# A two-block transformer on one NeuronCore: pool projections first on the unshifted input, the output projection in two halves, routing on the way

## The reference, cut to what matters

```python
ada = jax.nn.silu(c) @ w_ada[l] + b_ada[l]                    # 2048 x 12288 weights, one vector
sh1, sc1, gt1, sh2, sc2, gt2 = jnp.split(ada, 6, axis=-1)
h = modulate(rmsnorm(x, norm1_g[l]), sh1, sc1)                # xn * (1 + sc1) + sh1
proj = h @ w_in[l]
q, k, v, qi, ki, wi, p = jnp.split(proj, offsets, axis=-1)
q = rope_partial(rmsnorm(q, q_norm_g[l]), pos)                # 8 heads of 128; k has 2 heads
...
attn_out = dsa_attention(q, k, v, qi, ki, wi)                 # top-k of index scores masks the softmax
pool_out = multiscale_pool(p, w_pool[l], pool_scale[l])       # trailing mean minus identity, then a matmul
mix = jnp.concatenate([attn_out, pool_out], axis=-1) @ w_out[l]
x = x + gt1[:, None, :] * mix
h2 = modulate(rmsnorm(x, norm2_g[l]), sh2, sc2)
x = x + gt2[:, None, :] * hier_moe(h2, w_grp[l], w_exp[l], w1[l], w3[l], w2[l])
```

## Time and profile before

| | |
|---|---|
| median of three runs | 2413.72 us (2411.43 to 2416.28) |
| the profiled execution | 2411.38 us, its span 2409.1 us |
| TensorE busy | 2096.6 us (87%), mean granted clock 0.972 |
| VectorE, ScalarE busy | 1220.2 us (51%), 872.2 us (36%) |
| HBM read | 691.66 MB, 288 GB/s over the span |

### The profile page before, as it was taken

How to read it: one execution, slowest core, us unless ns; L and a number is a source line. 1 busy time by engine, 2 the same in 40 slices (tenths; PEclk the granted TensorE clock), 3 DMA queues, 4 the chain that set the end, 5 groups by cost and what they waited for, 6 DMA issues and landing times.

```text
span 2409.1 us, 38203 instructions
## 1 busy us (share of the span) xinstructions
PE 2096.6 (87%) x14478; PEld 1356.6 (56%) x14478; DVE 1220.2 (51%) x2209; ACT 872.2 (36%) x1339; POOL 32.8 (1%) x32
## 2 busy tenths in 40 slices
PE   5699998987988888888888888899989899997997
PEld 1377776872222222222222222798888899997887
DVE  1544786455443333333333333648865554477655
ACT  1333434442221111111111112547854444466543
POOL 0000000000000000000000000101100000000000
PEclk9899999998999999999999999999999999999998
DMA  9988785967999999999999999464345355543432
GB/s 383 403 313 295 256 291 201 320 233 287 422 422 422 422 422 422 422 422 422 422 422 422 422 422 420 148 232 140 123 149 183 123 175 184 176 147 101 139 127 93
DMA packets 135046, 695.44 MB, mean 289 GB/s; under 512 B 14992, under 2 KB 15120, under 8 KB 85264
## 3 DMA queue, kind: packets, MB, share of 16 engines
q1 hardware_dynamic: 134928, 693.81, 75.4%
HBM read 691.66 MB, written 2.10 MB: 288 GB/s over the span
## 4 chain that ended last, share of the span: by engine, by line
PE 50%; DMA 36%; DVE 6%; ACT 3%; issue 2%; SPq 2%; DVEq 0%; ACTq 0%
PE acc L1088 35%; DMA ring<-in_w 31%; DMA land<-in_stream_a 4%; PE acc L1085 3%; PE psS L1345 3%; PE psO L1139 2%; DVE WL L1793 1%; ACT WH L1499 1%; SPq L956 1%; DMA land<-in_stream_bc 1%; PE psM L1333 1%; PE acc L1333 1%; PE psT L1029 1%; ACT SB L1580 0%; PE psO L1369 0%
## 5 line engine op out<-in xcount | busy, mean ns | idle before, releaser
L1088 PE MATMUL acc<-HH,WH 128*128 128x256 f32 x2552 | 747.2, 293 | 32.9 <-DVE HL L1815 15.7
L1088 PE MATMUL acc<-HH,WL 128*128 128x256 f32 x2552 | 728.4, 285 | 0.0
L1088 PE MATMUL acc<-HL,WH 128*128 128x256 f32 x2552 | 727.8, 285 | 0.0
L1793 DVE TENSOR_TENSOR WL<-land,WH 128x1024 fp32r<-128x1024 f32 (+2 forms) x346 | 418.6, 1211 | 409.6 <-ACT WH L1499 405.3
L1088 PEld LDWEIGHTS acc<-HH,WH 128*128 128x128 f32 x2552 | 496.0, 194 | 75.2 <-issue 14.9
L1088 PEld LDWEIGHTS acc<-HH,WL 128*128 128x128 f32 x2552 | 496.4, 195 | 1.9 <-issue 1.0
L1088 PEld LDWEIGHTS acc<-HL,WH 128*128 128x128 f32 x2552 | 495.8, 194 | 0.0
L1499 ACT ACTIVATE WH<-land 128x1024 fp32r<-128x1024 f32 (+2 forms) x350 | 364.3, 1042 | 238.3 <-PE acc L1088 192.1
L1345 PE MATMUL psS<-ring,low 128*32 128x512 f32 x2048 | 276.6, 612 | 106.4 <-DMA ring<-in_w 105.4
L1345 PEld LDWEIGHTS psS<-ring,low 128*32 128x32 f32 x2048 | 40.8, 108 | 319.8 <-DMA ring<-in_w 289.7
L2172 DVE TENSOR_TENSOR X<-psM,X 128x512 f32<-128x512 f32 x128 | 88.5, 691 | 230.0 <-PE psM L1333 230.0
(11 more groups left out here) (343 smaller groups left out, 1899.0 us busy)
## 6 DMA issues: line engine op xcount, KB each, us to landing
ring<-in_w SPq DMA_DIRECT2D x384, 1024.0 KB, 26.5
land<-in_stream_a SPq DMA_DIRECT2D x284, 512.0 KB, 7.3
land<-in_stream_bc SPq DMA_DIRECT2D x246, 512.0 KB, 4.0
land<-in_stream_bc SPq DMA_DIRECT2D x12, 384.0 KB, 3.4
X<-in_xT SPq DMA_DIRECT2D x1, 2048.0 KB, 16.1
out<-low SPq DMA_DIRECT2D x4, 512.0 KB, 2.6
cst<-in_const SPq DMA_DIRECT2D x1, 1538.0 KB, 11.9
low<-in_w_pool SPq DMA_DIRECT2D x1, 1024.0 KB, 4.7
```

Of the source, the lines that this page charges most:

```text
L1088: mm = pe.matmul(bank[:, 0:S], w[:, kk, :], h[:, rows[kk], :], start=(z == 0 and i == 0), stop=stop)
L1793: ins = dve.tensor_tensor(wl, src, wh, ALU.subtract)
```

## The change

1. **ada order** is 4, 5, 6, 7, 0, 1, 2, 3, 8, ... (`ADA_FIRST`). After the four scale blocks and the sum of squares the eight pool projections run, on `HH0`/`HL0`: x times (1 + sc1) times gain, without the shift and without the token's norm. VectorE multiplies the token's norm into each result (`evac` of p); the shift adds the same to every position of a feature, which the pool maps to zero. Blocks 0 to 3 are spread among them, and `HH`/`HL` for the others are made meanwhile.
2. ki and wi share one projection (`kw`). The pool sums and `pmm` move among the qi projections.
3. The queries' norm is no longer multiplied into q: `qss` sums its squares into one column for each head, `qrms`/`qsqrt`/`qrec` are done once, and `soft` takes the result as a scale for each head (four instructions for each job in place of one).
4. `idx` uses two 64-row matmuls on one copy of the keys, into `psS`; one `idx` runs after the first half of a q projection, one after the second. Each `topk` is four steps of two rounds.
5. The output projection runs twice over all 16 outputs: first the pool half (`wp`), with the attention jobs among them, each result added to X, then the attention half (`wo`).
6. The router's weights are multiplied by the modulation (`cols`), and the logits are taken from the unnormed X after each `wo` (`logit`, 128x36), the norm and the shift's part (`shiftW`) being applied at the end. h2 is no longer made: `h2t` turns X, `pick` writes the token's norm into the choice matrix, and scale and shift are applied on the gathered tile by VectorE (`inputs`, two instructions of 512 elements in place of ScalarE's copy), in the loop too.
7. `place` ends before the list of tiles, which follows the first `pick`; `gt2rows` moves ahead of the last two `wo`. The first four `ring` slots are loaded as soon as the landing slots under them are free.

```diff
-    for b in range(8):
+    o.will_split([("p", n) for n in range(8)])
+    for g in range(4):
+        b = ADA_FIRST[g]
         for q in range(4):
...
+            if (g, q) == (3, 1):
+                first = o.halves_of["p", 0][0]
+                o.add("pe", "part", ("p", 0), 0)
...
+    for n in range(8):
+        o.proj(("p", n), between=shifts, first=int(n == 0))
...
+    for n in range(KD):
+        o.proj(("wp", n), halves=[o.halves_of["wo", n][0]], post="res", between=after if 0 < n < 14 else None)
+        if n == 0:
+            o.add("dve", "qrms")
+            o.add("act", "qsqrt")
+            o.add("dve", "qrec")
+        if n < 4:
+            topk(1, n)
+        if n in (2, 4, 6, 8):
+            o.job(n // 2 - 1)
+        if n == 13:
+            o.split_mix("wo", 0)
...
     for n in range(KD):
-        o.proj(("wo", n), post="res", between=after, first=int(n < 2))
+        o.proj(("wo", n), halves=[o.halves_of["wo", n][1]], post="res", between=last)
...
-    o.add("dve", "rstd", "wo")
-    o.acc.append(("router",))
-    for c in range(KD):
-        o.add("dve", "h2", c)
-        o.add("act", "h2", c)
-    o.add("dve", "gt2rows")
-    o.add("pe", "router")
-    o.add("act", "evac", ("router",))
-    o.add("pe", "routeT")
-    o.misc.append(("routeT",))
+    o.add("dve", "logits")
...
     o.add("dve", "place")
+    o.add("dve", "pick")
+    o.add("dve", "list")
+    o.add("dve", "weights")
...
+                        if name == "p":
+                            ins = dve.tensor_tensor(pooled(n // 2)[:, n % 2, :], bank[:, 0:S], RT, ALU.mult)
...
+            def inputs(i):
+
+                dve.wait_ge(moe["gt_full"], i + 1)
+                dve.tensor_tensor(XG, acc[1][:, :].rearrange("p (c n m) -> p c n m", c=4, m=CAP),
+                                  g2.rearrange("p (n c) -> p c n", c=4)[:, :, :, None].to_broadcast([P, 4, 4, CAP]),
+                                  ALU.mult).then_inc(moe["xg_half"], 1)
...
+                dve.tensor_tensor(XG, XG, sh2.rearrange("p (n c) -> p c n", c=4)[:, :, :, None].to_broadcast([P, 4, 4, CAP]),
+                                  ALU.add).then_inc(moe["xg_ready"], 1)
```

More of the change, by code:

```diff
@@ L413, in order_a @@
-    ada_t(7)
-    rest = [(("k", 0), "nr"), (("k", 1), "nr"), (("v", 0), None), (("ki", 0), "r"), (("wi", 0), None)]
-    rest += [(("qi", n), "r") for n in range(8)] + [(("q", n), "nr") for n in range(8)]
+            if g and q == 1:
+                scale_first(g - 1)
+            if g in (1, 2):
+                o.add("pe", "ssx", 4 * (g - 1) + q)
+            if (g, q) == (2, 3):
+                o.misc.append(("ssx", 7))
+                o.add("dve", "ssx", 7)
+                o.add("act", "sqrtx")
+                o.add("dve", "xr")
@@ new lines, in order_a, with topk, index, halfway @@
+    pool_at = {("kw", 0): 0, ("qi", 0): 1, ("qi", 2): 2, ("qi", 4): 3}
+    pmm_at = {("qi", 2): 0, ("qi", 4): 1, ("qi", 6): 2, ("qi", 7): 3}
+    def topk(qt, part):
+        o.add("dve", "topk", qt, part)
+    def index():
+        i = idx.pop(0)
+        o.add("pe", "idx", i)
+        o.add("act", "evac", ("idx", i))
+        o.add("dve", "idx", i)
+    def halfway(x):
+        calls = [0]
+        def step():
+            calls[0] += 1
+            if x != ("q", 7):
+                between()
+            if calls[0] == 1 and x[1]:
+                index()
+        return step if x[0] == "q" else between
@@ new lines, in order_a @@
+    for x, post in rest:
+        if x == ("q", 7):
+            while len(left) % 4:
+                ada(*left.pop(0))
+        o.proj(x, post=post, between=halfway(x))
+        if x in pool_at:
+            o.add("dve", "pool", pool_at[x])
+        if x in pmm_at:
+            for dc in range(2):
+                item = ("pmm", (pmm_at[x], dc))
+                o.add("pe", *item)
+                o.acc.append(item)
+                o.add("act", "evac", item)
+        if x[0] == "q":
+            index()
+            if x[1] >= 4:
+                topk(0, x[1] - 4)
@@ new lines, in order_a, with last @@
+    o.drain()
+    shared[0], owed[0] = False, 0.0
+    o.misc.append(("ssum", "wo"))
+    o.add("pe", "shiftW")
+    o.add("dve", "shiftW")
+    def last():
+        between(ADA_RATE[3])
+    for n in range(KD):
+        o.proj(("wo", n), halves=[o.halves_of["wo", n][1]], post="res", between=last)
+        if not left and ("adaT", 23) not in o.at["pe"]:
+            ada_t(23)
+            o.add("dve", "gt2rows")
+            o.add("pe", "gt2rows")
+            o.add("act", "gt2rows")
+    assert not left
@@ L737, in program @@
         X = sb("X", [P, KD, S])
+        low_at = (nc.sbuf_base + 31) // 32 * 32
         low = sb("low", [P, 48, S])
@@ L1702, in softmax_head @@
                         needs("pe", "T", jobs[n - 2])
+                    elif k == 0:
+                        needs("pe", "pmm", (3, 1))
                     if k == 0:
-                        scale, mask = P ** -0.5, W(aSC + qt)[:, 0, 0:nk]
+                        for h in range(4):
+                            at = 8 * qt + 4 * (j % 2) + h
+                            ins = dve.scalar_tensor_tensor(out=s[:, h, :], in0=psS[:, h, 0:nk], scalar=rqa[:, at:at + 1],
+                                                           in1=W(aSC + qt)[:, 0, 0:nk], op0=ALU.mult, op1=ALU.add)
+                        then(ins)
                     elif j[0] == "b":
@@ L1985, in run @@
                                                            op0=ALU.mult, op1=ALU.mult)
-                    elif what == "top1":
-                        needs("pe", "routeT")
-                        then(dve.tensor_copy(rt[:, 0:72], psM[:, 0:72]))
+                    elif what == "logits":
+                        needs("act", "sqrtn", "wo")
+                        then(dve.reciprocal(rtok, rsum))
+                        for tt in range(NT):
+                            ins = dve.scalar_tensor_tensor(out=LG[:, tt, :], in0=psM[:, 36 * tt:36 * tt + 36],
+                                                           scalar=rtok[:, tt:tt + 1], in1=shw, op0=ALU.mult, op1=ALU.add)
+                    elif what == "top":
                         gl = LG[:, :, 0:4]
```

548 lines of the change are left out of this document (301 added, 247 removed).

## The result

The changed kernel takes 2391.74 us in the median of five runs (2388.19 to 2393.90), the kernel before 2413.53 (2405.92 to 2416.28): a ratio of 0.9914, with a 95% interval of 0.9895 to 0.9934. It is faster by 0.9%, 22 us where 51 were forecast, and 2391.7 lies outside the range that ended at 2383. The span of the profiled execution went from 2409.1 to 2387.6 us.

A forecast was written before the change was run, and what follows sets the result against it. The expert loop was taken as bound by its weight loads, so stage A's length sets the end. Gains 17 + 1.4 + 13 + 19.5 = 51 us took the profiled 2411.4 us to 2360, median 2362; range 2345 to 2383.

The forecast's parts named there:

- The bound and the mechanism: Expert loop bound by its weight loads; whatever comes ahead of it, at 566.84 us, moves the rest one for one.
- three signs of being wrong: k after 140 us, TensorE waiting over 10 us for VectorE among `wp`, or loop bandwidth below 420 GB/s.
- A: Front, up to k's first product: k at 130 us with 16 pool halves run earlier, gain 17 us.
- B: TensorE work taken out or added behind the front: sum -1.4 us, nearly a draw.
- C: Waits, gaps and half clock from k to the last product: 33 us before, 20 left, gain 13 us.
- the first index score (3 us): Stage A: a TensorE wait at the first index score, expected to stay at 3 us.
- SP's new wait for w_pool on p(7) costs nothing: Load queue: it stands at piece 99, reachable only once piece 90 is used, behind p(7); no cost.
- the split of the pool half ahead of `wp`(0): Start of the output projection: a new wait of 4 us, since `HH` is in use until q(7) is done.
- Rival 2: VectorE binds around the change to `wp`, 31 us against TensorE's 25: 2377 us, chance 0.17.
- rival 1: Half clock in the front: k at about 150 us, gain 31 us, 2382 us, chance 0.10.
- D: Tail, last product to first w1 product: 25 us instead of 44.6, first gather at +15, gain 19.5 us.
- E: Expert loop and rest: about 1 us more on a tile of 24.67, loads take 29.8; no cost.

The follow-up runs named there:

- e12: Changed kernel with eight landing slots of 512 KB in stage A instead of nine: 2412.6 us.
- e13: Kernel before the change with eight landing slots in stage A instead of nine: 2419.97 us.
- e1: Changed kernel with the shift's logits product (`shiftW`) moved behind the fourth `wo` output instead of ahead of the first: 2384.9 us.
- e9: Changed kernel with k(1)'s rotation between the halves of qi(1) and the first index score waiting for qi(0)'s rotation, not qi(7)'s: 2386.0 us.
- e5: Changed kernel with w_pool loaded behind the pieces of qi(1) instead of those of wi(0): 2387.5 us.
- e2: Changed kernel with the split of the pool values ahead of the last index score and last step of the first top-k: 2389.9 us.
- e7: Changed kernel with the four steps of each top-k in one piece, behind `wp`(0) and `wp`(3): 2397.5 us.
- e3: Changed kernel with 28 products that nobody reads ahead of `wp`(0), to keep TensorE busy in its wait: 2392.3 us.
- e10: Changed kernel with the moves of e1, e2, e5 and e9 together: 2368.45 us, ratio 0.9826 against the kernel before.
- e6: Changed kernel with the list of tiles ahead of the first pick again on VectorE: 2390.6 us.
- e8: Changed kernel with four more VectorE instructions of 0.7 us ahead of `inputs` in every expert-loop tile: 2413.7 us.
- e14: Kernel of e10 with four ada units and their turn put ahead of `wp`(0): 2373.08 us, ratio 0.9839 against the kernel before.

## Why the prediction was right or wrong, step by step

**The bound and the mechanism** were read rightly: whatever stands ahead of the first w1 product moves the end one for one. 22.2 us came there, 21.5 in the span. Faster was forecast with 0.96. None of its three signs of being wrong came: k stood at 135.5 us and not behind 140, TensorE waited 2.8 us for VectorE among `wp` (6.9 with `shiftW` behind them) and not 10, and the loop kept its 422 GB/s. The sign that failed was the last product, "at about 490 us", at 521.57.

**A** (17, measured 11.7). The step that failed is "28.0 MB, at the 404 GB/s of the earlier trace rows". 404 was in the main the rate of a stretch in which the landing slots held ada pieces, which TensorE frees: 411 GB/s from 66 to 99.8 us, and 391 from there to 117, with the first halves. Now 18 of the 50 pieces ahead of k are halves, freed by VectorE's low part, and the rate is 360 and 379. SP's waits in the kernel before from 66 to 100 us, then in the changed kernel from 50 to 136 us:

```profile
SPq L923 <- PE psO L1139: 21.7, 13, 2.6
SPq L923 <- DVE WL L1793: 2.4, 1, 2.4
```

```profile
SPq L990 <- DVE WL L1914: 55.2, 18, 6.4
SPq L990 <- PE psO L1220: 3.5, 5, 1.1
```

The prediction gave TensorE's side and the DMA's side each a time and took the larger; with nine slots the two are coupled, as e12 and e13 show (9 us for one slot, none before). p's first product came at 53 instead of 60 us, which hid part of it: from there to k it was to be 70 us and was 82.3. That is luck, since the sum had no reason for an early p. "Granted clock near 1 from 65 us" was wrong: 0.93.

**B** was right to 1 us: what is neither a half projection nor an ada unit took 52.7 us of TensorE's timeline before and 58.2 now, 5.5 more where 4.5 were expected. The index scores took 8.5 us and not 7.2, the logits 7.1 as counted.

**C** failed, and with it the forecast: "I take 20", with 35 as the upper bound, where 46 was found. By its own list:
- Not on it at all: the wait of `shiftW` for `cols` on VectorE, new, 4.1 us long and worth 6.8 (e1). It stands in point 6 of the change, and the order of steps alone shows what is ahead of it on VectorE.
- "the first index score (3 us)" was on it, the rotation on a shared bank was not: 6.5 together (e9).
- "SP's new wait for w_pool on p(7) costs nothing": the wait, yes; its megabyte ahead of v's pieces 2.6 us (e5).
- "the split of the pool half ahead of `wp`(0)", put at 4 us, took 7.1, since the last rotation, two index sums and a top-k step stood ahead of it on VectorE. But half of it taken away gave only 0.6 (e2), so this half had almost no price.
- VectorE in the first five `wp`, put at 4 us: the waits there are 2.8, with the steps of the top-k worth 6.5 (e7). Rival 2 did not come; the steps, which it had counted in, are part of the reason.
- Half clock: rival 1 had the mechanism and the wrong place. It was priced for the front alone, with 0.10; it stands behind the waits of the whole stage, 1.5 us at the one where it was measured (e3), and the 15 us by which the halves of this stretch exceed their unit price are its upper bound there (12 before).

e10, which moves only steps of this list, gives back 17.3 of the 25.7 us by which B and C missed.

**D** (19.5, measured 21.8) was right up to the gather, at +15 (15.2). From there to the first w1 product it had 10 us and 7.9 were found, and the first w1 product came at +22.8 instead of +25: it had the list wholly on the chain on either side of the pick, and e6 shows about half of it hidden. (522.27 us, its end of the last product before, is the start of the last turn, 0.1 us off.)

**E** was right: a tile with its weights at hand takes 596.29 - 571.06 = 25.2 us instead of 24.67 (the w2 rows of two tiles), below what the loads take, and no cost can be read behind the first w1 product. But "5.1 us for each tile are free" was too simple: e8 used 2.8 of them and paid 22, of which 6.4 came with GpSimd's work at the loop's end.

**Open**: the remaining 8 us of C and the 5 of A. That they hang on the landing slots is likely and not shown: e12 shows what a slot less costs, and no run has a slot more. How much the pool projections first are worth alone was not tried. The single runs are one profile each.

## What to carry to other kernels

When work is moved to where an engine is free, list every step that waits across engines in the new order and ask what stands ahead of its producer in that producer's own queue: three such waits of 3 to 4 us, which no duration showed, were worth 13 us, where the work taken out was worth 1.4. Don't price a wait of TensorE by its length: those of `shiftW` and of the rotations, 4.1 and 4.9 us taken away, gave 6.8 and 6.5, slow products included, while 3.5 and 3.6 us taken from the one ahead of `wp`(0) gave 0.6 and 1.0 (e2, e14). Try the move. Useless products in a wait made those behind it fast (e3), but the run gained nothing by it, since they took longer than the wait. Where loads land in a few slots, don't cost a stretch as the larger of load time and compute time: see who frees a slot, and how late that engine is.

## What the runs showed of the hardware that was not expected

Not every wait is followed by slow products. In the changed kernel those of 2.92, 3.50, 4.13 and 7.11 us are, those of 2.29 and 2.39 are not; in the kernel before the one of 3.13 us at 403 was not, and the one of 2.61 at 416 was, so the length of a wait alone does not tell. The wait of the same step, 2.39 us in the changed kernel and 2.38 in e2, was followed by products 0.12 us apart in the one and, from the eighth on, 0.21 in the other. Where they come, they end after 3 to 5 us of products 0.21 us apart. The waits for VectorE in the loop of e8 (59.8 us in 24 tiles of the window) lowered its granted clock from 0.99 to 0.92, so that TensorE's busy time for the same products rose from 574.9 to 609.7 us: a wait that the loads should have hidden made the work itself longer.

VectorE instructions were longer while GpSimd ran. In e8, while GpSimd ran its low parts (2.34 to 2.67 us each), VectorE instructions that took 0.35 us in all tiles of the changed kernel took up to 2.50 us, and in the changed kernel two of 0.48 us (`HL`, L1928, at 1490 and 1492.5) took 1.73 while GpSimd ran. No run was made on this alone.
